# Moving waits inside the tiles of a two-layer recurrent decoder step, and sharing its two ends with GpSimd

## The chip, the cores and the metric

The kernel runs on one core of a Trainium2 chip. The metric is device time in microseconds (us), the median of several executions. All data starts and ends in HBM.

## The reference, cut to what matters

One inference step of a two-layer decoder trunk runs for a prompt of 512 tokens and for 8 samples of 4 tokens, 544 tokens in all, with model width 1024 in float32. Each layer adds half a SwiGLU block, then a mixer, then half a SwiGLU block:

```python
x = x + 0.5 * _swiglu(_rmsnorm(x, norm_ffn1), w_ffn1_in, w_ffn1_out)          # width 2816
xn = _rmsnorm(x, norm_mix)
(mq, mk, mv, mo, mg_if, gq, gk, gv, gg, glr, lx, ly, mgate) = _split_cols(xn @ w_in)
h_ml, C1, n1, m1 = _mlstm(q, k, v, log_i, log_f, C0, n0, m0)                  # 4 heads, chunks
y_ml = _head_layernorm(h_ml, g_ml_norm) * sigmoid(mo)
o_gla, S1 = _gla(gq_, gk_, gv_, _heads(log_a, GLA_HEADS), S0)                 # 4 heads
y_gla = _head_rmsnorm(o_gla, g_gla_norm) * silu(gg)
xc, cb1 = _causal_conv(lx, cb0, w_conv, b_conv)
h_lru, h1 = _rglru(xc, w_lru_a, b_lru_a, w_lru_i, b_lru_i, lru_lambda, h0, pos)
y_lru = h_lru * gelu(ly)
merged = gm[:, :, 0] * y_ml + gm[:, :, 1] * y_gla + gm[:, :, 2] * y_lru       # gm = sigmoid(mgate)
x = x + merged @ w_out
x = x + 0.5 * _swiglu(_rmsnorm(x, norm_ffn2), w_ffn2_in, w_ffn2_out)
```

A last RMSNorm follows. All recurrent states are outputs too.

## The kernel before, in words

Activations lie transposed: 8 feature tiles (k) of 128 partitions by 544 tokens. A weight block of 128x2048 is loaded by SyncE's queue into one of two slots of `stage`; ScalarE (ACT) writes its rounded high part `wh` (L776), VectorE (DVE) writes the rest `wl` (`split_lo`, L1075), and the block is free for the next load. TensorE (PE) makes a product of high and low parts in three passes (L393). `tile` (L399 on) runs 8 k-steps of 6 matmuls into one of two PSUM pairs, `stream_a` and `stream_b`; DVE evicts a tile with `take` (L1066, L1068), which multiplies by `rstd`, the reciprocal norm, and so can run only when the norm of the tokens is done. A tile of the same pair may start only after that eviction. PSUM `mix` (Q, 4 banks) holds all small products.

Every engine's order is written out by hand, and semaphores join them. `link` makes DVE wait for its own last instruction. Per layer, in this order:

- **ffn** (two halves of up and down tiles). After it comes the **gate block** (`gate_block`, `gate_rows`, L1176 on): a tile of gate columns, the column sums of squares (`norm_squares`, L425), and then `q`, `k` and value tiles of the first head. DVE evicts the gate tile with `rstd`.
- **mLSTM heads** (`mlstm_head`), 4 of them. Near the end of a head PE runs `mean` (`column_sum`, L520, which waits for `a_h`, the sum `wS`) between k-steps 2 and 3 of the last tile, then the variance sum (L520 on `hsq`, which waits for `square_sum`, L1281) after it. ACT's `head_root` (L866) follows, and `merge_head` (L1288 to L1295) in the next head.
- **GLA heads** (`gla_head`), 4 of them. The first starts with `decays` (L615), which waits for the last mLSTM head's root. DVE turns 14 slices `seven` into factors (L1433) once ACT has made the exponentials, and takes the values (L1219) in the middle of that. At the end of a head PE runs `sample_updates` (L513) and the variance sum after the last tile, waiting for `square_sum`.
- **LRU pairs** (`lru_pair`), 4 of them: convolution (L1509 to L1530), gates (L719), a scan (`recur`), GeLU branch (`take_y`), and `merge` (L1578 to L1582) of the pair before. Its state inputs reuse memory of the heads, so their loads wait until the last GLA state is stored.
- **out blocks**, 4 of two tiles, which read `mh` and `ml`, the merged result; k-steps wait for `m_ready`.
- **ffn** again. After layer 2: last norm (L425, L806, L1099), 8 scalings (L1640) and 8 stores.

At the start ACT makes high parts and squares of x in turn, DVE low parts and the running sum `acc`, with the first two weight blocks' parts between them; GpSimd (POOL) sets constants and issues 21 small loads. The layer loop of PE is a hardware loop (`Fori`).

## Time and profile before

| | us |
|---|---|
| median of 3 executions | 3292.69 (3290.55 to 3293.36) |
| the profiled execution | 3291.07 |
| its span, first to last instruction | 3288.9 |
| PE busy, 24,724 matmuls | 3155.8 (96%) |
| DVE busy | 1929.6 (59%) |
| ACT busy | 1027.3 (31%) |
| GpSimd busy | 11.4 (0%) |

PE is the bound nearly everywhere: what the other engines do counts only where PE waits for them, at the start before its first matmul and at the end after its last. The profile also gives the clock that PE was granted: 0.98 of full speed over the span, with stretches at half speed.

### The profile page before, as it was taken

Reading aid. Unit: us, or ns where it says so; the run is one execution under the profiler, and the core shown is the slowest. Engines: PE = TensorE matmul, PEld = TensorE weight load, DVE = VectorE, ACT = ScalarE, POOL = GpSimd, SP = SyncE. Lnnn points to the kernel's source line nnn. Section 1 sums busy time; section 2 is a strip of 40 time slices with the busy share of each in tenths; the row PEclk is TensorE's granted clock in tenths of the full one; section 3 lists DMA queues with packets and bytes.
Section 4 is the critical chain, followed back from the end, with each engine's and each line's share of the span. In section 5 each row is a group of like instructions: output and inputs, shape, how many; then the busy total and the mean of one; then the engine's idle time right before and its main releaser. Section 6 shows DMA issues by size and latency. Waiting matters only on the chain.

```text
span 3288.9 us, 58471 instructions
## 1 busy us (share of the span) xinstructions
PE 3155.8 (96%) x24724; PEld 3098.9 (94%) x24724; DVE 1929.6 (59%) x2653; ACT 1027.3 (31%) x983; POOL 11.4 (0%) x33
## 2 busy tenths in 40 slices
PE   7999989999999999999999999999999999999997
PEld 7999989989889989999999999899898899899997
DVE  5434467667777875434454345666777788654344
ACT  3222232333334543212232123232333346421122
POOL 1000000000000000000000000000000000000000
PEclk9999999999999999999999999999999999999999
DMA  4232232322222222222222223232222222222221
GB/s 143 80 102 81 78 106 94 126 92 79 79 91 75 83 79 81 77 98 84 83 90 85 99 80 99 77 136 91 92 79 78 86 89 77 77 90 83 96 75 67
DMA packets 52021, 292.53 MB, mean 89 GB/s; under 512 B 9480, under 2 KB 12296, under 8 KB 23992
## 3 DMA queue, kind: packets, MB, share of 16 engines
q1 hardware_dynamic: 37440, 243.60, 22.2%
q10 hardware_dynamic: 13696, 46.32, 3.9%
q8 instruction: 86, 1.41, 0.2%
q0 software_dynamic: 768, 0.95, 0.1%
q14 instruction: 31, 0.25, 0.0%
HBM read 269.33 MB, written 21.50 MB: 88 GB/s over the span
## 4 chain that ended last, share of the span: by engine, by line
PE 67%; DVE 18%; ACT 8%; issue 3%; DMA 3%; DVEq 0%; ACTq 0%; SPq 0%
PE stream_b L393 30%; PE stream_a L393 30%; PE stream_a L467 3%; ACT wh L776 2%; DVE wl L1075 2%; DMA out_o_ss<-CS 2%; DVE hsq L1288 2%; DVE xc L1524 1%; DVE seven L1433 1%; PE stream_b L467 1%; PE mix L647 1%; DVE tg L1360 1%; DVE tg L1066 1%; ACT L987 1%; DVE Cst L1264 0%
## 5 line engine op out<-in xcount | busy, mean ns | idle before, releaser
L776 ACT ACTIVATE wh<-stage 128x2048 fp32r<-128x2048 f32 (+2 forms) x246 | 436.0, 1772 | 837.6 <-PE stream_b L393 549.3
L1075 DVE TENSOR_TENSOR wl<-stage,wh 128x2048 fp32r<-128x2048 f32 (+2 forms) x248 | 525.9, 2120 | 161.3 <-ACT wh L776 144.9
L393 PE MATMUL stream_a<-xh,wh 128*128 128x272 f32 x2560 | 542.5, 294 | 29.6 <-DVE wl L1075 15.8
L393 PE MATMUL stream_b<-xh,wh 128*128 128x272 f32 x2560 | 537.2, 291 | 9.3 <-DVE lyg L1066 7.0
L393 PE MATMUL stream_a<-xh,wl 128*128 128x272 f32 x2560 | 534.8, 291 | 0.0
L393 PE MATMUL stream_a<-xl,wh 128*128 128x272 f32 x2560 | 532.8, 290 | 0.0
L393 PE MATMUL stream_b<-xh,wl 128*128 128x272 f32 x2560 | 528.7, 288 | 0.0
L393 PE MATMUL stream_b<-xl,wh 128*128 128x272 f32 x2560 | 527.7, 287 | 0.0
L393 PEld LDWEIGHTS stream_a<-xh,wh 128*128 128x128 f32 x2560 | 408.8, 192 | 34.2 <-issue 19.2
L393 PEld LDWEIGHTS stream_b<-xh,wh 128*128 128x128 f32 x2560 | 402.4, 188 | 17.4 <-DVE lyg L1066 7.8
L393 PEld LDWEIGHTS stream_a<-xh,wl 128*128 128x128 f32 x2560 | 408.8, 191 | 0.0
L393 PEld LDWEIGHTS stream_a<-xl,wh 128*128 128x128 f32 x2560 | 406.2, 191 | 0.0
L393 PEld LDWEIGHTS stream_b<-xh,wl 128*128 128x128 f32 x2560 | 402.7, 189 | 0.0
L393 PEld LDWEIGHTS stream_b<-xl,wh 128*128 128x128 f32 x2560 | 400.3, 189 | 0.0
L1066 DVE TENSOR_TENSOR us<-stream_b,rstd 128x544 f32<-128x544 f32 x88 | 63.8, 725 | 446.2 <-PE stream_b L393 446.2
L827 ACT ACTIVATE sg<-gs 128x544 f32<-128x544 f32 x88 | 57.9, 658 | 398.2 <-DVE gs L1066 398.2
L467 PE MATMUL stream_a<-wh,xh 128*128 128x256 f32 x512 | 144.6, 282 | 6.1 <-DVE qT L1066 6.1
L393 PE MATMUL stream_b<-hh,wh 128*128 128x272 f32 x704 | 146.1, 289 | 0.0
L393 PE MATMUL stream_a<-hh,wh 128*128 128x272 f32 x704 | 146.0, 289 | 0.0
L467 PE MATMUL stream_a<-wh,xl 128*128 128x256 f32 x512 | 145.4, 284 | 0.0
L393 PE MATMUL stream_a<-hh,wl 128*128 128x272 f32 x704 | 145.3, 287 | 0.0
L393 PE MATMUL stream_b<-hh,wl 128*128 128x272 f32 x704 | 145.2, 287 | 0.0
(331 smaller groups left out, 4586.5 us busy)
## 6 DMA issues: line engine op xcount, KB each, us to landing
stage<-in_w_up SPq DMA_DIRECT2D x88, 1024.0 KB, 4.9
stage<-in_w_mix SPq DMA_DIRECT2D x88, 1024.0 KB, 4.9
stage<-in_w_down SPq DMA_DIRECT2D x32, 768.0 KB, 4.3
stage<-in_w_down SPq DMA_DIRECT2D x32, 640.0 KB, 3.9
CS<-in_c ACTq DMA_DIRECT2D x8, 1024.0 KB, 4.7
out_o_sc<-CS ACTq DMA_DIRECT2D x8, 1024.0 KB
CS<-in_s ACTq DMA_DIRECT2D x8, 1024.0 KB, 4.9
out_o_ss<-CS ACTq DMA_DIRECT2D x8, 1024.0 KB
```

What stands on the lines that cost most here:

```text
L393: mm = [pe.matmul(out(h), a(h), b(h), start=f, stop=z) for h in range(2)]
L467: mm = pe.matmul(out, a[:, k, tok:tok + C], b[:, j, k * DV:(k + 1) * DV], start=f, stop=z)
L647: mm = pe.matmul(Q[:, q, sl], lhs, rhs, start=True, stop=True)
L776: act.activation(wh[:, slot, 0:width], stage[:, slot, 0:width], ACT.Copy).then_inc(hi_done, 1)
L827: act.activation(sg[:], gs[:], ACT.Silu).then_inc(silu_done, 1)
L987: act.activation(lyg[:, v, :], lyg[:, v, :], ACT.Gelu_apprx_tanh).then_inc(l_act, 1)
L1066: ins = tt_(halves(dst), banks(pair[slot]), rs2, ALU.mult)
L1075: tt_(wl[:, slot, 0:width], stage[:, slot, 0:width], wh[:, slot, 0:width].bitcast(F32), ALU.subtract).then_inc(split_done, 1)
L1288: link(dve.reciprocal(hsq[:, 1, :], hsq[:, 1, :]))
L1360: link(dve.reciprocal(tg[:], tg[:]))
L1433: tt_(ev[:, :, a, :], ev[:, :, a, :], sv[:, :, a, :], ALU.mult)
L1524: stt(xc[:, j, 0:T], lxp[:, j, a:a + T], w[a], xc[:, j, 0:T], ALU.mult, ALU.add)
```

## The change

It keeps the mathematics and moves work:

- **Start.** Both halves of x load on ACT's queue. ACT makes the high part of weight block 0 first, then high parts and squares in groups, and block 1's high part last. DVE makes block 0's low part first and then all 8 low parts of x; the squares of k 0 to 3 are summed by GpSimd, which also makes block 1's low part. The norm's column sums move into the middle of the second tile. `ones` is set by GpSimd instead of loaded.
- **Gate block.** DVE copies the gate tile raw to `sq` before the norm is known, clears `val` and `Kf` while it waits, and takes `q` before the gate logarithms are back. ACT makes the next block's high part before the rows' store.
- **Heads.** In `mlstm_head` one `split_lo` moves behind `a_h`, `mean` runs ahead of the last tile, and the variance sum after its k-step 5; ACT's root runs before the last gate. The reciprocal of `merge_head` becomes `invert_root` and moves to the next head's start (mLSTM) or ahead of the wait for the exponentials (GLA). In `gla_head` the merge moves ahead of the second gate, a `split_lo` behind the states, `evictions` into the third gate, and three `sample_updates` and the variance sum into the last tile.
- **LRU.** `take_y(1)` runs before `recur(0)`. In the last pair of a layer each half is merged as soon as it is ready, and `split(4)` comes last.
- **End.** No high and low parts are made in the last ffn. ACT scales rows 0 to 2 of x by the final weight and loads the square root's table early; GpSimd multiplies these three rows by `rstd`, DVE the other five.
- PE's layer loop is written out for both layers.

The diff, cut to its core:

```diff
@@ gpsimd
+            for e, m in enumerate((1, 2, 3)):
+                pool.wait_ge(sq_ready, m + 1)
+                pool.tensor_tensor(first_sum, first_sq[0] if m == 1 else first_sum, first_sq[m], ALU.add).then_inc(first_half, 1)
...
+            pool.tensor_tensor(wl[:, 1, :], stage[:, 1, :], wh[:, 1, :].bitcast(F32), ALU.subtract).then_inc(split_done, 1)
...
+            pool.wait_ge(last_norm, 1)
+            for m in range(3):
+                pool.tensor_tensor(x[:, m, :], y_part[m][:], rstd[:], ALU.mult).then_inc(y_pool, 1)
@@ tensor, mlstm_head
-                pair_block(n + 3, t + 6, 1, None, ((), ((2, mean), (7, third))))
-                pe.wait_ge(a_sqs, B + 1)
-                column_sum(hsq[:, 0], 0, a_var)
+                pair_block(n + 3, t + 6, 1, mean, ((), ((5, variance), (6, third))))
@@ tensor, gla_head
-                pair_block(n + 3, t + 6, 1, outputs)
-                pe.wait_ge(b_sqs, B + 1)
-                sample_updates(1, 2, b_us)
-                pe.wait_ge(head_samples, taken + 1)
-                sample_updates(2, 3, b_us)
-                column_sum(hsq[:, 0], 0, b_var)
+                def second():
+                    pe.wait_ge(b_h, B + 1)
+                    sample_updates(1, 2, b_us)
+
+                def third():
+                    pe.wait_ge(b_sqs, B + 1)
+                    column_sum(hsq[:, 0], 0, b_var)
+                    pe.wait_ge(head_samples, taken + 1)
+                    sample_updates(2, 3, b_us)
+
+                pair_block(n + 3, t + 6, 1, outputs, ((), ((4, second), (6, third))))
@@ tensor
-            with pe.Fori(0, DEPTH) as L:
+            for L in range(DEPTH):
@@ scalar, mlstm_head
+                act.wait_ge(a_var, B + 1)
+                head_root()
                 next(gates, None)
                 split_hi(nh + 2, 1, t + 7, 2 * D)
-                act.wait_ge(a_var, B + 1)
-                head_root()
@@ vector, gla_head
                 split_lo(n + 2, 0, 2 * D)
+                invert_root(number - 1)
                 dve.wait_ge(b_exp, B + 1)
...
+                merge_head(HEADS - 1 if first else i - 1, first)
                 take_gate(L, i, t + 5, 1, 1, acts + 1, "silu", None)
-                split_lo(n + 4, 0, 2 * D)
@@ vector, lru_pair
+                take_y(1)
+                recur(0)
+                if not last:
...
+                else:
+                    take(t + 4, 0, tt[:, 0])
+                    split(3)
+                    merge(0)
+                    take(t + 5, 1, last_branch)
+                    recur(1)
+                    merge(1)
+                    split(4)
```

PE, the end of a GLA head of the middle (`xh,wh`, `xl,wh` and `xh,wl` matmuls of `stream_b` are its last tile, `mix<-V4,Kws` the sample updates, `mix<-hsq,ones` the variance sum; what waits stands in brackets). Before:

```order
L393 MATMUL stream_b<-xh,wh 128x272 x2
L393 MATMUL stream_b<-xh,wl 128x272 x2
L393 MATMUL stream_b<-xl,wh 128x272 x2
L513 MATMUL mix<-V4,Kws 128x256 [waits b_square_sum]
L513 MATMUL mix<-V4,Kws 128x256
L700 ISA
L513 MATMUL mix<-V4,Kws 128x256 [waits head_samples]
L513 MATMUL mix<-V4,Kws 128x256
L520 MATMUL mix<-hsq,ones 128x272 x2
L703 REGISTER_ALU
L513 MATMUL mix<-V4,Kws 128x256 [waits head_samples]
```

And now, from k-step 4 of that tile on:

```order
L544 MATMUL mix<-V4,Kws 128x256 [waits b_h]
L544 MATMUL mix<-V4,Kws 128x256
L410 MATMUL stream_b<-xh,wh 128x272 x2
L410 MATMUL stream_b<-xh,wl 128x272 x2
L410 MATMUL stream_b<-xl,wh 128x272 x2
L410 MATMUL stream_b<-xh,wh 128x272 x2
L410 MATMUL stream_b<-xh,wl 128x272 x2
L410 MATMUL stream_b<-xl,wh 128x272 x2
L551 MATMUL mix<-hsq,ones 128x272 [waits b_square_sum]
L551 MATMUL mix<-hsq,ones 128x272
L738 REGISTER_ALU
L544 MATMUL mix<-V4,Kws 128x256 [waits head_samples]
```

The wait for the squares stood after all 8 k-steps and now stands after 6, with a wait for `b_h` ahead of k-steps 5 and 6.

DVE, the middle of an mLSTM head, from the eviction of its second gate tile to that of its third (`wl<-stage,wh` is the low part of the next weight block, `wS<-Hh` the sum that PE's `mean` waits for). Before:

```order
L1066 TENSOR_TENSOR tg<-stream_b,rstd 128x544 [waits tile_done]
L1075 TENSOR_TENSOR wl<-stage,wh 128x2048 [waits hi_done,gate_act,tile_free]
L1358 SCALAR_TENSOR_TENSOR tg<-mix,seven 128x512 [waits a_denominator]
L1359 TENSOR_TENSOR tg<-tg,mix 128x512 [waits dve_chain]
...
L1366 TENSOR_TENSOR Hh<-mix,tg 128x2x512 [waits a_out,dve_chain]
L1367 TENSOR_TENSOR wS<-Hh 128x544 [waits dve_chain]
L1066 TENSOR_TENSOR tg<-stream_a,rstd 128x544 [waits tile_done]
```

And now:

```order
L1128 TENSOR_TENSOR tg<-stream_b,rstd 128x544 [waits tile_done]
L1435 SCALAR_TENSOR_TENSOR tg<-mix,seven 128x512 [waits a_denominator,gate_act,tile_free]
L1436 TENSOR_TENSOR tg<-tg,mix 128x512 [waits dve_chain]
...
L1443 TENSOR_TENSOR Hh<-mix,tg 128x2x512 [waits a_out,dve_chain]
L1444 TENSOR_TENSOR wS<-Hh 128x544 [waits dve_chain]
L1137 TENSOR_TENSOR wl<-stage,wh 128x2048 [waits hi_done]
L1128 TENSOR_TENSOR tg<-stream_a,rstd 128x544 [waits tile_done]
```

The low part of the weights moved from ahead of the denominator to between `wS` and the third gate tile.

## Rows read from the trace of the kernel before

**Rows 1.** PE's waits: us in total, times, longest us.
```profile
PE mix L513 <- DVE hsq L1281: 33.4, 8, 5.0
PE stream_a L393 <- DVE wl L1075: 15.8, 1, 15.8
PE mix L520 <- DVE wS L1367: 10.7, 6, 1.9
PE stream_a L393 <- DVE ml L1582: 10.5, 4, 3.5
PE stream_a L393 <- DVE val L1219: 9.2, 5, 4.3
PE mix L615 <- ACT hsq L866: 8.5, 2, 4.3
PE stream_b L393 <- DVE lyg L1066: 7.0, 4, 1.8
PE stream_a L467 <- DVE qT L1066: 6.1, 2, 3.1
...
PE stream_b L393 <- DVE xg L1183: 2.3, 2, 1.2
```

**Rows 2.** Windows behind long waits: length, busy (count) by engine, PEclk, DMA; sums.
```profile
866.00:869.93 3.93, 3.93 (x13) 3.46 (x14) 2.47 (x5) 3.87 (x5) 0.00 (x0) 0.50 0.00 0
...
sum 38.31, PE 38.30 PEld 34.57 DVE 29.02 ACT 36.18 POOL 0.00; mean PE 4.79 PEld 4.32 DVE 3.63 ACT 4.52 POOL 0.00
...
sum 11.11, PE 11.11 PEld 11.11 DVE 8.63 ACT 3.47 POOL 0.00; mean PE 3.70 PEld 3.70 DVE 2.88 ACT 1.16 POOL 0.00
...
sum 12.10, PE 12.10 PEld 10.45 DVE 5.83 ACT 3.15 POOL 0.00; mean PE 6.05 PEld 5.22 DVE 2.91 ACT 1.57 POOL 0.00
...
sum 18.61, PE 15.03 PEld 14.40 DVE 12.82 ACT 2.59 POOL 0.00; mean PE 7.52 PEld 7.20 DVE 6.41 ACT 1.29 POOL 0.00
```

**Rows 3.** Timeline of the start: start, duration, instruction, idle before and releaser.
```profile
0.91 0.15 POOL L360 MEMSET pick<- 128x64 f32 x1
...
11.28 1.91 ACT L793 ACTIVATE wh<-stage 128x2048 fp32r<-128x2048 f32 x1 [0.94 <-DMA stage<-in_w_up]
...
27.31 1.08 PE L425 MATMUL mix<-acc,ones 128*128 128x272 f32 x4
...
33.35 0.72 DVE L1066 TENSOR_TENSOR gs<-stream_a,rstd 128x544 f32<-128x544 f32 x1 [0.38 <-DVE rstd L1099]
```

**Rows 4.** Timeline of the gate block, DVE.
```profile
461.18 2.29 DVE L1075 TENSOR_TENSOR wl<-stage,wh 128x2048 fp32r<-128x2048 f32 x1 [10.19 <-ACT wh L776]
```

**Rows 5.** Timeline of the second mLSTM head, ACT.
```profile
636.79 1.11 ACT L909 ACTIVATE hsq<-Hh 128x1088 f32<-128x1088 f32 x1 [2.45 <-DVE Hh L1371]
```

**Rows 6.** Timeline of the first two GLA heads, DVE.
```profile
740.24 1.23 DVE L1219 TENSOR_TENSOR val<-stream_a,rstdT 128x1024 f32<-128x1024 f32 x1 [1.53 <-PE stream_a L467]
...
853.73 3.55 DVE L1288 RECIPROCAL hsq<-hsq 128x544 f32<-128x544 f32 x1
```

**Rows 7.** Timeline where a layer's LRU pairs begin and end, DVE.
```profile
1038.87 0.18 DVE L1514 COPY lxs<-cv 128x24 f32<-128x24 f32 x1 [3.54 <-DMA cv<-in_conv]
...
1190.89 1.29 DVE L1546 TENSOR_TENSOR_SCAN hseq<-xg,ii 128x544 f32<-128x544 f32 x1
...
1204.28 0.72 DVE L1582 TENSOR_TENSOR ml<-tt,mh 128x544 fp32r<-128x544 f32 x1
```

**Rows 8.** Timeline of the end, ACT and DVE.
```profile
3271.06 0.64 ACT L815 ACTIVATE sq<-x 128x544 f32<-128x544 f32 x1
...
3274.89 1.28 ACT L806 ACT_TABLE_LOAD   x1 [3.19 <-PE mix L425]
...
3280.76 5.66 DVE L1640 SCALAR_TENSOR_TENSOR x<-x,vectors,rstd 128x544 f32<-128x544 f32 x8
```

**Rows 9.** DMA queue (packets, MB, share) and an issue (KB each, us to landing).
```profile
q8 instruction: 86, 1.41, 0.2%
...
vectors<-in_vec SPq DMA_DIRECT2D x1, 112.0 KB, 2.3
```

More of the change, by code:

```diff
@@ L293, in trunk @@
         rr, aa = sd, (sq, xg)
-        first_sq = (sq, xg)
+        last_branch = xc[:, 0, :]
+        first_sq = [merged[:, m, :] for m in range(KT)]
+        first_sum = qT[:]
+        y_part = (gs, us, sg)
+        raw = sq
         def halves(ap):
@@ L360, in _ @@
             pool.memset(pick[:], 0.0)
+            pool.memset(ones[:], 1.0)
             pool.memset(one_t[:], 1.0).then_inc(split_done, 2)
@@ L410, in tile @@
                         late(k_tiles - 1 - k)
+                    if low is not None:
+                        pe.wait_ge(low, k + 1)
                     if fresh is not None:
@@ L426, in norm_squares, with first_block @@
                 return mm
+            def first_block(n, t, j, norm):
+                parts = (wh[:, j], wl[:, j])
+                block_ready(n)
+                tile(t, 0, KT, 2 * P, 0, weights=parts, low=first_low)
+                tile(t + 1, 1, KT, 2 * P, P, weights=parts, ks=range(KT // 2))
+                pe.wait_ge(acc_ready, norm)
+                norm_squares().then_inc(norm_sum, 1)
+                tile(t + 1, 1, KT, 2 * P, P, weights=parts, ks=range(KT // 2, KT))
             def ffn_in_block(L, n, t, j, norm=None):
+                if norm == KT:
+                    return first_block(n, t, j, norm)
                 block_ready(n)
@@ L599, in mean, with variance @@
                     sample_updates(1, 3, a_us)
+                def variance():
+                    pe.wait_ge(a_sqs, B + 1)
+                    column_sum(hsq[:, 0], 0, a_var)
                 def third():
@@ L843, in down @@
                             if half == 1:
-                                squares(i * 2 + (t + j), i * 2 + j, g_col + i * 2 + j)
+                                squares(i * 2 + (t + j), i * 2 + j, g_col + i * 2 + j, not last)
                             if width:
@@ L967, in lru_pair, with branch, gates @@
                 t = L * LAYER_TILES + i * 12 + (TILE_MIX + GATE_TILES + 2 * HEADS * HEAD_TILES + 6 * j2)
-                def gates(j):
+                def branch(v, buf):
+                    tile_taken(t + 4 + v)
+                    act.activation(buf, buf, ACT.Sigmoid).then_inc(l_act, 1)
+                def gates(j, between=None):
                     k = pr * 2 + j
@@ L1046, in _ @@
             chain.end()
+            for m in range(3):
+                high = (DEPTH - 1) * V_COLS + V_NEXT + m
+                act.wait_ge(h_done, DEPTH * 2 * sum(FF_HALVES))
+                act.activation(y_part[m][:], x[:, m, :], ACT.Copy,
+                               scale=V[:, high:high + 1]).then_inc(xh_ready, 1)
+            act.activation(sdT[:], sdT[:], ACT.Sqrt)
             norm_root(3 * DEPTH)
@@ L1138, in down @@
                             if half == 1:
-                                prepare(i * 2 + j, g_col + i * 2 + j, norm * KT + i * 2 + (KT + j))
+                                prepare(i * 2 + j, g_col + i * 2 + j, norm * KT + i * 2 + (KT + j), not last)
                             if width:
@@ L1589, in mix @@
                 dve.wait_ge(tile_free, L * LAYER_TILES + (TILE_MIX + 3))
+                tile_ready(L * LAYER_TILES + (TILE_MIX + 1))
+                dve.tensor_copy(halves(raw[0:80]), banks(pair[1])[0:80]).then_inc(tile_free, 1)
+                dve.wait_ge(tile_free, L * LAYER_TILES + (TILE_MIX + 4))
+                chain.restart()
+                link(dve.memset(val[:, :, DV:DV + P], 1.0))
+                link(dve.memset(val[:, NC, 0:DV], 0.0))
+                link(dve.memset(Kf[:], 0.0))
                 reciprocal_norm(L * 3 + 1)
```

193 lines of the change are left out of this document (109 added, 84 removed).

## The prediction

> **What bounds the kernel now.** I read the busy times first: PE works for 96% of the span, so an edit pays only where PE stands still or runs slowly. The next view is PE's waits [rows 1]. The nine rows sum to 103.5 us, from a few places that repeat per head or per layer: 33.4 us in eight waits for the sum of squares at the end of a GLA head, 10.7 in six waits of `mean` in an mLSTM head, 8.5 in two for the root before `decays`, 17.6 in the gate block and the values behind it, and 17.5 among the LRU pairs and the out blocks. Third, windows laid behind the long waits [rows 2]. The reader is to see the granted clock in the first one: 0.50, the 1.2 GHz level, although PE is busy throughout. Behind each wait of about 3 us or more PE shows such a stretch, behind the waits of under 2 us in the heads none. So a long wait costs its length and half of the busy time behind it: 38.31/2 = 19.2 us behind the eight GLA waits, 11.11/2 = 5.6 in the gate block, 12.10/2 = 6.0 behind `decays`. By PE's busy time over its 24,724 matmuls (0.128 us each) a k-step, which is 6 matmuls, takes 0.75 us at full clock, a tile 6.0, and I take 1.4 for a k-step at half. Last I read the timelines of the places that the change touches, engine by engine [rows 3 to 8], and followed each new order of DVE, ACT and PE with the durations of those rows. Against the profiled execution (3291.07 us) the sum is:
>
> **A, the start: +1.1.** Before, block 0 landed at 11.28 and ACT wrote `wh` at once, since its table had been loaded under x [rows 3]. Now the table load (1.28, as in [rows 8]) and `wh` (1.9) follow the landing, then DVE's low part (2.29 [rows 4]) and the first low part of x (0.8): PE starts at 17.6 instead of 15.8 [rows 1]. Twelve k-steps later, three of them at half clock, the norm's column sums start at 28.4 instead of 27.31. From there to the first eviction it took 6.04 us [rows 3]; the third tile waits for that, so the delay of 1.1 stays. If block 0 lands between the halves of x, 2.6 us sooner, this is -1.5; if x and the block share the queue badly, +3. Block 1's low part goes to GpSimd; its only price here is a memset of 64 columns in 0.15 us [rows 3], or 4.8 us for 2048 columns, and it has over 10 us until block 1 is used.
>
> **B, the gate block: -21.3.** The raw copy frees the tile's PSUM without the norm, and `q` is taken before the rows are ready. The waits for xg (2.3), qT (6.1) and the values' eviction (4.3 and 3.0 of the 9.2) go [rows 1], and 5.6 of half clock [rows 2]: 15.7 + 5.6. The clears of `val` and `Kf` fill the time in which DVE waits for the norm, and ACT's `wh` no longer stands behind the rows, for which DVE's low part waited 10.19 us [rows 4]. In my replay `q` is out 9 us before PE needs its slot and the values in time.
>
> **C, mLSTM heads: +4.2.** The low part (2.29) and its wait move behind `wS`, so `mean` loses its 10.7 us [rows 1]. But the variance sum moves from behind k-step 8 to behind k-step 5. Behind `wS` DVE and ACT need: low part 2.29 [rows 4], and, as each operation over 544 columns takes about 0.7 [rows 7, 8], eviction, sigmoid and product with two hand-overs 1.65 from the eviction's start, centring 1.35 (two of them), square 1.11 [rows 5], square sum 0.73: 7.1. PE needs 1.5 for `mean` and 5 x 0.75 for the k-steps, 5.3, and arrives about 1.86 us early, in all eight heads: +14.9 - 10.7. None of these waits is long enough for half clock. Queued behind the waiting sum are three k-steps and `third`, which has slack. Bounds: 0 (DVE is quicker, -10.7 in all) and 3.0 a head with half clock behind it (+20).
>
> **D, `decays` and the first GLA head: -2.1.** ACT's root now runs ahead of the last gate, so the 8.5 us go [rows 1] and 6.0 of half clock [rows 2]. What is late next: DVE in that head has the reciprocal (3.55 [rows 6]) ahead of the exponentials, which it formerly had later. Before, DVE waited 1.53 us for the values' tile at 740.24 [rows 6]; now PE is about 4.3 us earlier, while DVE has 3.55 more to do and only its 2.3 of idle time ahead of the factors to cover it. The eviction comes some 4.2 us late, in each layer, with about 2.0 of half clock: +12.4. Bounds 0 and 6 a layer.
>
> **E, the GLA heads: -54.5.** The variance sum moves from behind k-step 8 to behind k-step 6, which sounds like a later wait for PE, but DVE's squares move further: the merge, with its reciprocal of 3.55 [rows 6] and two products, leaves the place just ahead of the third gate tile, the `split_lo` too. In the replay the squares are ready at 65.6 us of a head and PE asks for them at 67.8. All 33.4 us go [rows 1], 19.2 of half clock [rows 2], and 1.9 of the waits for the values in the heads of the middle (0.80, 0.64 and their like in layer 2). The margin of the values' eviction there is thin, 0.25 us.
>
> **F, LRU and out blocks: -9.6.** Here a chain over DVE and ACT sets the time of a pair, PE has slack. (1) The last GLA state is stored some 2.2 us later against PE, and the loads of the pairs start behind it; DVE waited 3.54 for them already [rows 7]: +2.2. (2) `take_y(1)` stands ahead of `recur(0)`: +0.76 for three pairs. (3) In the last pair 12.8 us lay between the end of the last scan (1190.89 + 1.29) and the end of the second `ml` (1204.28 + 0.72) [rows 7]. Now one merge of 3.75 follows it; merge(0) stands ahead of the scan with one eviction, 3.75 + 0.76 less an idle 2.4: the scan ends 2.1 later. So `ml` is ready 6.65 earlier, and PE has 1.9 less to do behind it (one k-step of two tiles instead of two). Per layer 2.2 + 2.3 - 8.55 = -4.1, two layers -8.1. PE was busy 15.03 us at half clock there [rows 2]; 1.5 of it goes with the waits for `ml` (10.5 [rows 1]), while those for `lyg` (7.0) stay or grow. Bounds: -22 (all waits for `ml` and their half clock) and 0.
>
> **G, the end: -3.4.** No high part: ACT's square, which ended at 3271.70 [rows 8], is 0.65 earlier. ACT then scales three rows (3 x 0.65) and loads the table (1.28 [rows 8]) beside PE's sums; the root starts at 3274.65, not 3276.18: -1.5. DVE scales five rows, not eight, of 0.70 each (5.66/8 [rows 8]): -2.1. GpSimd has three products in the same time. Their price by the memset is between 0.6 us (a fixed 0.1 and 0.9 ns a column) and 1.3 (0.15/64 a column); at 1.3 the three take 3.8 instead of 3.5: +0.2.
>
> **PE's written-out loop: 0.** No wait of PE's shows the engine looking for instructions.
>
> Sum: 1.1 - 21.3 + 4.2 - 2.1 - 54.5 - 9.6 - 3.4 = -85.6, so 3205.5 against the profiled execution. The median of the runs is 1.6 above that execution: **3207 us**.
>
> **The rivals.** *GpSimd and DVE exclude each other.* If a product with two inputs in SBUF on one of them stops the other, the eight scalings at the end run one after the other, 5 x 0.70 + 3 x 0.6 to 1.3, or 5.3 to 7.4 for the 5.66 of before, and the start's sums and low part stretch by 1 or 2: 3207 + 3.5 = **3210.5**. For it: both use the same memory at the same time, against it: nothing in this trace, where GpSimd does no such work. The Trainium skill, page "SBUF — State Buffer", section "Who interferes with whom", speaks against this part of the change: a DVE instruction with two inputs in SBUF contends with a GpSimd instruction that reads it, through a port pair that one of them locks. No row here can show it. Chance 0.2.
>
> *DVE becomes the bound of the GLA heads.* With PE's 8 us a head gone, DVE is left with 0.25 us of margin at the values. If each operation costs a few ns more than I counted, a wait of 2 us appears in six heads, with 1.3 of half clock: +20, **3227**. For it: the values' waits of before (0.80, 0.64); against it: the replayed order still has idle time in DVE. Chance 0.13.
>
> *The new waits of C, D and F do not appear*, because PE meets them later than replayed: -14.9 (I keep 4), -12.4 (I keep 8): **3192**. Chance 0.13.
>
> *PE's code is fetched too late*, the slower side. The layer loop is written out, so PE passes through twice the code. The instruction queue carried 86 packets [rows 9]. If every packet of as many new ones stalls PE for a small load's time to landing, 2.3 us [rows 9], that is 198 us: **3403**. It decides from 85.6/86 = 1.0 us a packet on, above which the kernel is slower than before. Against it: the inner loops remain, and the long written-out stretches of PE today show no such gap. The Trainium skill, page "Runtime: NRT & Kernel Launch", section "Instruction fetch mechanics", holds the other way: streaming ahead is mostly hidden, and taken branches break it. The trace agrees as far as it goes, with no wait of that kind. Chance 0.02.
>
> *A part does not do what it says*: the long waits of the GLA heads return elsewhere, half of E is lost, 3207 + 27 = **3234**. Chance 0.04.
>
> **How the numbers follow.** The forecast's own case has 0.48, with bounds from A (-2.6 to +1.9), C (-10 to +10), D, F (-5 to +5), about 12 either way together. To 8 in 10 the range takes in the cases of GpSimd, of DVE's bound and of the waits that do not appear: **3186 to 3230**. What a measurement of this kernel can tell from no change is about 0.2%, 6.6 us. All cases but the slower side lie far under 3286: faster 0.96, same 0.02, slower 0.02.
>
> **What would show it.** PE's waits of the changed kernel should have no line for the sample updates behind `hsq`, none for xg or qT, eight waits of about 1.9 us at the variance sum of the mLSTM heads, two of about 4 at the values of the first GLA heads, waits for `lyg` as before and none or short ones for `ml`. PE's first matmul comes at 17.6. Windows in the GLA heads should show a granted clock of 1.0. At the end five scalings of DVE stand beside three products of GpSimd, and their durations, against 0.70, tell whether the two exclude each other. I would be wrong if PE's total wait were above 60 us, if a GLA head took over 72 us instead of 70.5 (78.5 before), or if PE showed gaps without a releaser.

## The result, and the profile after

The changed kernel takes 3237.72 us (median of 4 executions, 3237.12 to 3239.91); the kernel before takes 3291.62 (4 executions beside them). The ratio is 0.9838, 95% interval 0.9821 to 0.9855: 1.6% faster. The forecast was 3207, with a range of 3186 to 3230. The sign is right, the time lies 7.7 us above the range, and of the 85.6 us that were forecast 53.7 came.

| | before | after |
|---|---|---|
| the profiled execution | 3291.07 | 3237.12 |
| its span | 3288.9 | 3235.2 |
| PE busy | 3155.8 | 3134.7 |
| PE's idle time before its last matmul | 119.0 | 84.7 |

The page's busy times after the change:

```profile
PE 3134.7 (97%) x24724; PEld 3083.5 (95%) x24724; DVE 1928.0 (60%) x2638; ACT 1034.0 (32%) x987; POOL 26.5 (1%) x40
```

PE's waits after the change (us in total, times, longest):

```profile
PE stream_a L410 <- DVE xl L1143: 18.6, 2, 17.9
PE stream_a L410 <- DVE val L1292: 15.4, 8, 4.2
PE mix L551 <- DVE hsq L1356: 14.9, 8, 2.1
PE stream_b L410 <- DVE tt L1128: 6.8, 4, 2.2
PE stream_a L410 <- DVE lxs L1587: 6.5, 2, 3.2
PE stream_a L410 <- DVE x L1157: 5.6, 4, 2.7
PE mix L443 <- DVE acc L1237: 3.1, 1, 3.1
PE stream_a L410 <- DVE gs L1128: 2.5, 1, 2.5
...
PE stream_a L410 <- DVE ml L1654: 1.4, 2, 0.7
```

Beside [rows 1] the reader sees what the change does: the lines of 33.4, 10.7, 8.5, 6.1 and 2.3 us are gone, and that of `ml` is down from 10.5 to 1.4. In their place stand the variance sum of the mLSTM heads (14.9, eight times, as forecast), the values in eight GLA heads where two were forecast (15.4), and the waits of LRU and out blocks for `tt`, `lxs` and `x` (18.9 together), of which the forecast had little; the 7.0 us for `lyg`, which it left standing, are gone. PE's whole idle time of 84.7 us lies above the 60 that the prediction named as a sign of being wrong, and a middle GLA head takes 71.6 us from value tile to value tile, where it had 70.5.

PE's order of tile matmuls is the same in both kernels, so the start of the same tile in both traces can be subtracted. These differences, cut at the borders of the stages, give the sum as measured (a border can be drawn a few tenths of a us to either side):

| term | forecast | measured |
|---|---|---|
| A, start, to the third tile | +1.1 | +7.05 (34.24 to 41.29) |
| B, gate block, two layers | -21.3 | -20.1 |
| C, mLSTM heads 1 to 3 | +4.0 | +5.8 |
| C to E, last mLSTM head, `decays`, GLA heads | -56.4 | -47.8 |
| F, LRU and out blocks | -9.6 | +3.2 |
| turn of the layer loop | 0 | -1.8 |
| G, end | -3.4 | -0.05 |
| sum | -85.6 | -53.7 |

### The profile page after: what moved, and what is told of

Its sections match the earlier page's. It is cut to its first block, busy times and chain, and to the rows that moved or that the text cites. A ratio compares the mean times of both kernels' runs of the same rounds, so it can differ in the third digit from the quotient of the medians.

```text
span 3235.2 us, 58231 instructions
## 1 busy us (share of the span) xinstructions
PE 3134.7 (97%) x24724; PEld 3083.5 (95%) x24724; DVE 1928.0 (60%) x2638; ACT 1034.0 (32%) x987; POOL 26.5 (1%) x40
## 4 chain that ended last, share of the span: by engine, by line
PE 71%; DVE 17%; ACT 6%; issue 3%; DMA 3%; DVEq 0%; ACTq 0%; POOL 0%; SPq 0%; POOLq 0%
PE stream_b L410 32%; PE stream_a L410 30%; DVE wl L1137 2%; PE stream_a L497 2%; DMA out_o_ss<-CS 2%; ACT wh L817 1%; DVE hsq L1362 1%; DVE seven L1512 1%; DVE tg L1437 1%; DVE xc L1602 1%; PE mix L680 1%; ACT L1038 1%; DVE tg L1128 1%; PE mix L551 1%; PE stream_b L497 1%
## 5 line engine op out<-in xcount | busy, mean ns | idle before, releaser
L410 PE MATMUL stream_a<-hl,wh 128*128 128x272 f32 x704 | 145.1, 287 | 0.0
L410 PE MATMUL stream_b<-hl,wh 128*128 128x272 f32 x704 | 145.0, 287 | 0.0
```

Source lines behind the costliest of these rows:

```text
L410: mm = [pe.matmul(out(h), a(h), b(h), start=f, stop=z) for h in range(2)]
```

## The experiments

Unless said otherwise, each is the changed kernel (3237.72 us) with the edit shown, and stands on one profiled execution; the differences by stage come from subtracting tile starts as above. At places that follow a stretch of half clock, steps of about 1.6 us come and go between runs whose code is the same there, so totals of single runs are read to about 2 us and the places by themselves.

### Start on DVE alone, and the end one engine after the other

```diff
-            for e, m in enumerate((1, 2, 3)):
-                pool.wait_ge(sq_ready, m + 1)
-                pool.tensor_tensor(first_sum, first_sq[0] if m == 1 else first_sum, first_sq[m], ALU.add).then_inc(first_half, 1)
...
-            pool.tensor_tensor(wl[:, 1, :], stage[:, 1, :], wh[:, 1, :].bitcast(F32), ALU.subtract).then_inc(split_done, 1)
@@ start, vector
+            for m in range(1, KT):
+                dve.wait_ge(sq_ready, m + 1)
+                ins = tt_(acc[:], first_sq[0] if m == 1 else acc[:], first_sq[m], ALU.add)
...
+            split_lo(1, 1, 2 * D)
@@ end, vector
+            dve.wait_ge(y_pool, 3)
             for m in range(3, KT):
```

> The changed kernel with two edits far apart. Start: GpSimd's three sums and its low part of block 1 are made by DVE. End: DVE waits until GpSimd's three products are done and only then scales its five rows. Theory A (an instruction of GpSimd and one of DVE that both read two inputs in SBUF exclude each other): at the start the low parts of x take 0.79 us each instead of 1.13, no sum takes 5 us, and the third tile starts near 36.4 instead of 41.29, so about -4.9; at the end GpSimd's products take clearly less than the 1.8 us of the changed kernel, about 1.1 to 1.3, and DVE's 0.70. Theory B (GpSimd is simply slow and DVE waits for its results, without exclusion): DVE's low parts stay at 1.13 us, the third tile starts at 39 or later, and GpSimd's products stay at 1.8 us alone.

Measured: 3236.75 us. The third tile starts 5.15 us sooner. Of this 1.5 are lost again at once: PE waits 2.76 us ahead of that tile instead of 2.48, and the 4.5 us behind the wait are at a granted clock of 0.62 instead of 1.00; 2.8 are left at the last tile. At the end 2.3 us are lost to the waiting. First the changed kernel's rows, DVE and GpSimd at the start (start, duration, instruction, idle time before):

```profile
16.97 9.03 DVE L1143 SCALAR_TENSOR_TENSOR xl<-x,vectors,xh 128x544 fp32r<-128x544 f32 x8
...
26.67 5.74 DVE L1235 TENSOR_TENSOR acc<-acc,merged 128x544 f32<-128x544 f32 x2
...
26.08 4.99 POOL L377 TENSOR_TENSOR wl<-stage,wh 128x2048 fp32r<-128x2048 f32 x1 [1.35 <-issue]
```

and at its end:

```profile
3225.16 6.79 DVE L1734 SCALAR_TENSOR_TENSOR x<-x,vectors,rstd 128x544 f32<-128x544 f32 x5
3225.28 1.86 POOL L399 TENSOR_TENSOR x<-gs,rstd 128x544 f32<-128x544 f32 x1 [3183.97 <-DVE rstd L1730]
3227.11 1.80 POOL L399 TENSOR_TENSOR x<-us,rstd 128x544 f32<-128x544 f32 x1
```

The same in this run, start and end:

```profile
17.16 5.66 DVE L1137 SCALAR_TENSOR_TENSOR xl<-x,vectors,xh 128x544 fp32r<-128x544 f32 x8
...
23.49 4.58 DVE L1229 TENSOR_TENSOR acc<-acc,merged 128x544 f32<-128x544 f32 x6
...
3223.78 1.32 POOL L393 TENSOR_TENSOR x<-us,rstd 128x544 f32<-128x544 f32 x1
...
3226.50 3.57 DVE L1731 SCALAR_TENSOR_TENSOR x<-x,vectors,rstd 128x544 f32<-128x544 f32 x5 [4.17 <-POOL x L393]
```

Alone, a product of GpSimd takes 1.32 us and a scaling of DVE 0.71 (3.57 for five). Side by side the products take 1.80 to 1.86, and of the five scalings the three that meet a product take 1.85 each, the first and the last 0.78 (the records of one instruction overlap the next by some 0.07). The two sums in 5.74 us are not stretched alike: the one that starts at 26.67, while GpSimd makes the low part of block 1 (26.08 to 31.07), takes 4.98 us, the next one 0.72. Without GpSimd six take 4.58. Three of the eight low parts of x, too, take 1.88 to 1.95 us beside GpSimd's sums, the other five 0.78. Theory A holds. The three products and five scalings one after the other are 3.96 + 3.57 = 7.53 us of work, together they took 6.79, and DVE had made eight in 5.66 [rows 8]. So GpSimd's help is worth less than nothing here. The Trainium skill, page "SBUF — State Buffer", section "Who interferes with whom", calls the port pair that the two engines share "an exclusive lock". The trace agrees: the sum of 4.98 us ends 0.58 us behind GpSimd's low part. That 6.79 is under 7.53 shows that a little of two such instructions is still overlapped.

### CS loaded behind the exponentials, and the end on DVE alone

```diff
@@ scalar, gla_head
-                act.wait_ge(state_stored, stored)
-                act.dma_start(CS[:], s0[L, i]).then_inc(b_cs, 16)
                 split_hi(nh + 1, 0, t + 1, 2 * D)
                 act.wait_ge(b_diff, B + 1)
...
                 act.activation(kh[:], kh[:], ACT.Exp, scale=inv).then_inc(b_exp, 1)
+                act.wait_ge(state_stored, stored)
+                act.dma_start(CS[:], s0[L, i]).then_inc(b_cs, 16)
@@ end, vector
-            for m in range(3, KT):
+            for m in range(KT):
```

At the end the three scaled rows of ACT and the three products of GpSimd go; the early load of the square root's table stays.

> The changed kernel with two edits far apart. GLA heads: ACT's wait for the stored state and its load of the next CS move from ahead of the high part of the weights to behind the four exponentials. End: DVE scales all 8 rows, GpSimd none. Theory A (the waits for the values in the second to fourth GLA heads, 2.0, 0.9 and 0.8 us a layer, come from ACT's queue, which stands still for the store before it makes wh, after which DVE's low part, reciprocal and factors follow): DVE's low part starts up to 3.7 us earlier and all six waits vanish, -7.1 us; the first heads' waits of 4.1 stay or shrink. Theory B (DVE's own work is the bound there): the waits stay within 0.5 us. End, by exclusion: 8 scalings in 5.66 instead of 6.79, and the end about 1.3 us shorter; without exclusion it would be longer, as three rows more are on DVE.

Measured: 3220.64 us, 17 us less. In the changed kernel the second GLA head reads, ACT and then DVE:

```profile
792.88 0.35 ACTq L1007 DMA_DIRECT2D out_o_ss<-CS  x1
803.02 0.33 ACTq L980 DMA_DIRECT2D CS<-in_s  x1
803.46 1.92 ACT L817 ACTIVATE wh<-stage 128x2048 fp32r<-128x2048 f32 x1 [12.10 <-DMA out_o_ss<-CS]
...
805.41 2.29 DVE L1137 TENSOR_TENSOR wl<-stage,wh 128x2048 fp32r<-128x2048 f32 x1 [3.70 <-ACT wh L817]
...
813.30 1.22 DVE L1292 TENSOR_TENSOR val<-stream_a,rstdT 128x1024 f32<-128x1024 f32 x1
```

and in this run:

```profile
798.50 1.92 ACT L812 ACTIVATE wh<-stage 128x2048 fp32r<-128x2048 f32 x1 [7.00 <-PE stream_b L405]
...
801.99 2.29 DVE L1127 TENSOR_TENSOR wl<-stage,wh 128x2048 fp32r<-128x2048 f32 x1
...
3210.48 5.66 DVE L1724 SCALAR_TENSOR_TENSOR x<-x,vectors,rstd 128x544 f32<-128x544 f32 x8
```

The store of the last state, 10 us from issue to landing, held up ACT's whole queue, `wh` among it; with the load moved, `wh` is made 5 us sooner and DVE does not wait for it. The line of the values in PE's waits goes from 15.4 us in eight to 8.6 in two, those of the first heads: six waits vanish, as theory A said. By the tile starts the heads give 13.7 us, about twice the 7.1 of the waits alone. The granted clock behind these waits was 1.00, so half clock is not the rest; it comes at the level matmuls behind them (L680 of the changed kernel), where six more waits for DVE, 2.0 us in all, go too, and in smaller steps around them. The end is 3.0 us shorter than the changed kernel's: 1.1 by the scalings, 1.2 because ACT no longer has three rows to scale ahead of the table and the root, and 0.7 between the last scaling and the end of the last store.

### The reciprocal at the merge again

```diff
@@ vector, gla_head
                 split_lo(n + 2, 0, 2 * D)
-                invert_root(number - 1)
                 dve.wait_ge(b_exp, B + 1)
...
+                invert_root(number - 1)
                 merge_head(HEADS - 1 if first else i - 1, first)
```

> The changed kernel with the reciprocal of the root back just ahead of the merge in the GLA heads. Theory A (the 3.55 us reciprocal ahead of the factors is what makes the values late): the waits for the values of 4.1 us in the two first GLA heads shrink to under 0.7, with some 2 us of half clock each, and those of the later heads vanish: together -18 us, unless the reciprocal makes the merge and the squares late, which would show as a wait at the variance sum or the sample updates in the last tile. Theory B (the values wait for something else, the exponentials of ACT): the waits stay above 3 us in the first heads.

Measured: 3246.41 us, 9 us more. PE's waits:

```profile
PE mix L530 <- DVE seven L1464: 13.1, 6, 2.9
PE stream_a L410 <- DVE val L1292: 10.7, 8, 2.4
```

The first heads' waits for the values shrink from 4.2 to 2.4 (2.2 in layer 2), not to under 0.7: the reciprocal is only part of it. In the later heads the 3.55 us delay the states, and the sample outputs (L530) wait for them. What stands ahead of the values in the first head is then ACT: DVE waits 1.54 us for the last of the exponentials, and six of its factors come before the eviction. The place of the change is the better one in three heads of four, the worse one in the first.

### The variance sum behind k-step 7

```diff
-                pair_block(n + 3, t + 6, 1, mean, ((), ((5, variance), (6, third))))
+                pair_block(n + 3, t + 6, 1, mean, ((), ((6, third), (7, variance))))
```

> The changed kernel with the variance sum of the mLSTM heads behind k-step 7 of the last tile instead of 5 (the third sample update stays behind 6). Theory A (PE is early at k-step 5 by 1.9 us and only the place is at fault): two k-steps of 0.75 cover 1.5 of 1.86, eight waits of 0.4 remain, -12 us, and nothing is late behind it. Theory B (the root that follows then is late for the next head's reciprocal or for the decays, or the sum waits for DVE wherever it stands): less than -6 us.

Measured: 3222.21 us, 15.5 us less. The line of `hsq` in PE's waits is gone altogether; in layer 1 each head is 1.74 us shorter, no line of waits is new (that of `ml` is 2.8 us instead of 1.4), and the first GLA heads wait 4.7 for the values instead of 4.2, since PE comes sooner. Even the 0.4 us that theory A left do not show. The 14.9 us of C were a choice of place, not a price of the new order.

### The state stored first, acc cleared early

```diff
@@ vector, gla_head (last head)
-                split_lo(n + 5, 1, 2 * D)
                 sample_states(eb, 3, 2, b_us, B, number)
+                split_lo(n + 5, 1, 2 * D)
@@ vector, mix
                 link(dve.memset(lxp[:, :, 0:3], 0.0))
+                link(dve.memset(acc[:], 0.0))
...
-                clear_acc()
```

> The changed kernel with two edits in the LRU part. In the last GLA head DVE updates the last sample states ahead of the low part of the weights, so that ACT can store the state sooner, behind which the pairs' loads wait; and acc is cleared ahead of the pairs instead of between the last merge and the first residual of the out blocks. Theory A (the LRU part starts late because the store is issued late, and the out blocks wait for work of DVE behind the last merge): the store is issued about 1.2 us sooner, as ACT's root is then the last thing ahead of it, the wait at lxs shrinks from 3.2 to about 2.0, and the wait at x in the out block from 2.65 to 1.6: -4 to -6 us in the two layers with their half clock. Theory B (the store takes until another transfer is done, whenever it is issued): the wait at lxs stays at 3.2.

Measured: 3234.39 us, 3 us less, of which the tile starts put 1.8 at the two places of the edit. The store is issued at 1004.66 instead of 1006.30 and the loads behind it at 1014.69 instead of 1015.83, although this run is 1.4 us behind the changed kernel here; DVE's wait for the loads (`lxs<-cv`) falls from 3.04 to 0.59 us. The store took 10.0 us instead of 9.5; a 1 MB weight block is loaded at the same time in the changed kernel, and the two move 2.1 MB in those 9.5 us. What the store would take by itself no run shows.

PE's wait at `lxs`, however, goes only from 3.2 to 3.0, and neither theory has the reason. The changed kernel's rows of DVE show it, and one of ACT (the issue of the first load):

```profile
1003.19 2.29 DVE L1137 TENSOR_TENSOR wl<-stage,wh 128x2048 fp32r<-128x2048 f32 x1 [1.02 <-ACT wh L817]
...
1007.80 3.55 DVE L1362 RECIPROCAL hsq<-hsq 128x544 f32<-128x544 f32 x1 [0.21 <-DVE Hh L1571]
...
1012.71 1.29 DVE L1372 TENSOR_TENSOR merged<-merged,Hh 128x1088 f32<-128x1088 f32 x1
...
1015.02 0.18 DVE L1587 TENSOR_TENSOR lxs<-stream_a,rstd 128x32 f32<-128x32 f32 x1
1018.24 0.18 DVE L1592 COPY lxs<-cv 128x24 f32<-128x24 f32 x1 [3.04 <-DMA cv<-in_conv]
...
1015.83 0.35 ACTq L1081 DMA_DIRECT2D h0t<-in_h  x1
```

PE waits from 1012.02 to 1015.25 for L1587, the last piece of the first LRU tile's eviction. That ends before the loads are even issued, so it can't wait for them: ahead of it stands the merge of the last GLA head, with its reciprocal, and DVE is busy nearly without a pause. The loads hold up DVE only behind it (L1592), where PE does not wait. In this run DVE no longer waits 1.0 us for `wh`, since the states come first, but the clearing of `acc` stands ahead of the eviction and takes 0.7 of it back. The wait at `x` goes from 2.65 to 2.0, half of what was expected.

### The eviction of the GeLU branch behind the scan

```diff
-                take_y(1)
+                if last:
+                    take_y(1)
                 recur(0)
                 if not last:
+                    take_y(1)
                     split(3)
```

> The changed kernel with the eviction of the second GeLU branch behind the first scan again in the three first LRU pairs of a layer, as before the change. Theory A (the pairs are set by the chain over DVE and ACT, and that eviction stands in it): each of three pairs is 0.76 us shorter, -4.6 in all, and the waits for lyg of 1.7 us come back in place of those for tt. Theory B (PE's wait for lyg is what the order was changed for, and weighs more): the pairs are longer by 0.5 to 1 us each, +3 to +6.

Measured: 3230.50 us, 7 us less. The LRU pairs and the out blocks are 3.0 and 2.7 us shorter in the two layers, 0.9 to 1.0 a pair. The waits for `tt` (6.8) are gone, one for `lyg` of 1.75 a layer is back. The rest of the 7 us comes up at places where the code is the same. The eviction stands in the chain that sets a pair's time, as the forecast had it (0.76 a pair).

### The start of before, and PE's loop

In the first of two runs ACT again makes high part and square of each row in turn and DVE low part and sum, with block 0 behind row 1 and the norm sums behind the first tile. The second also has

```diff
@@ tensor
-            for L in range(DEPTH):
+            with pe.Fori(0, DEPTH) as L:
```

> The changed kernel with the start of the kernel before: x on two queues, high part, square, low part and sum in turn on ACT and DVE, block 0 between them, norm sums behind the first tile, no arithmetic on GpSimd. Theory A (the new start is what costs 7.05 us at the third tile, in three parts: the first matmul 2.07 later, GpSimd and DVE excluding each other 4.9): the third tile starts at 34.24 again, and the whole run is 7 us shorter than the changed kernel. Theory B (part of it comes back later, since block 1 is ready earlier or later): the whole run differs from the start by over 1 us.

> Run e7 (the changed kernel with the start of before), with PE's layer loop as a hardware loop again. Theory A (the written-out loop costs and gives nothing): the run stands within 1.5 us of e7's 3229.25, no stage between the third tile and the end moves by over 0.5 us apart from steps of about 1.6 us that follow half clock. Theory B (it hides a fetch or costs one): a step of 1 us or more at the end of layer 1 or within layer 2.

Measured: 3229.25 us without and 3229.02 with the loop. With the old start the third tile starts 6.82 us sooner and the last tile 8.1: the new start costs what it seemed to and gives nothing back later; the 1.3 us more at the last tile are within the steps of half clock. The loop's run has a wait that the other has not, at the first matmul of layer 2:

```profile
1615.49 0.79 PE L405 MATMUL stream_a<-xh,wh 128*128 128x272 f32 x2 [2.01 <-issue]
```

The kernel before has it too, at the same matmul, where the profile puts it down to DVE:

```profile
1646.06 0.52 PE L393 MATMUL stream_a<-xh,wh 128*128 128x272 f32 x2 [1.72 <-DVE x L1088]
```

So the one turn of the hardware loop costs PE 1.7 to 2.0 us here, and writing the loop out gives that once. In the totals it is lost: the loop's run had about 4 us less of waits for the values. The rival in which the written-out code starves PE is refuted; the changed kernel's waits of PE have no line at issue. The Trainium skill, page "Runtime: NRT & Kernel Launch", section "Instruction fetch mechanics", names taken branches as what breaks the fetching ahead. The gap at the branch, and none in the straight code, agree with it; that the gap is a fetch no row says.

### The reciprocal behind the factors

```diff
                 split_lo(n + 2, 0, 2 * D)
-                invert_root(number - 1)
...
                 dve.memset(t8[:], 0.0).then_inc(b_fac, 1)
                 split_lo(n + 3, 1, 2 * D)
+                invert_root(number - 1)
```

with the load of CS as above.

> Run e2's edit in the GLA heads (ACT's load of CS behind the exponentials), without its end, and the reciprocal of the root not ahead of the factors but behind them and the next low part, ahead of the fifth gate tile, where DVE had 1.7 us of idle time. Theory A (in the first GLA head of a layer only the place of the reciprocal makes the values late, and this place has idle time): the values' waits of 4.2 vanish with 2 us of half clock each, and against e2 the heads are 10 to 12 us shorter. Theory B (the 3.55 us delay the ring of levels, the merge and the states, as in the run with the reciprocal at the merge): waits of 1.5 to 3 us appear at the level matmuls or at the sample outputs, in all heads, and the gain is gone.

Measured: 3253.02 us, 15 us more than the changed kernel. PE's waits:

```profile
PE mix L680 <- DVE wS L1529: 21.6, 8, 3.7
...
PE stream_a L410 <- DVE val L1292: 4.4, 2, 2.2
```

The values' waits in the first heads are halved, and in all eight heads the level matmuls now wait 2.1 to 3.7 us for DVE. The 1.7 us of idle time at that place were no slack: the ring of levels begins there, and everything behind it moves. Theory B.

### The last pair of a layer as before

```diff
                 else:
-                    take(t + 4, 0, tt[:, 0])
                     split(3)
-                    merge(0)
-                    take(t + 5, 1, last_branch)
+                    take(t + 4, 0, tt[:, 0])
                     recur(1)
-                    merge(1)
+                    take(t + 5, 1, tt[:, 1])
                     split(4)
+                    merge(0)
+                    merge(1)
```

ACT's order of the branches and PE's wait ahead of two k-steps follow it.

> The changed kernel with the last LRU pair of a layer as before the change: both merges behind both scans and behind the last low part, and PE waits for them ahead of the last two k-steps. Theory A (the two-step merge gives 6.65 + 1.9 us at the second ml and costs 2.65 and half clock at the next residual, which waits for the low part behind it): the pair and the out blocks are 9 to 11 us longer up to the second ml, the wait for x of 2.65 is gone, and the net is +4 to +7 a layer. Theory B (the two-step merge gives nothing net): within 1 us a layer.

Measured: 3248.45 us, 11 us more. Up to the end of the first two out tiles, where the second `ml` has been used, the layers are 9.9 and 10.0 us longer, behind the out blocks 5.1 and 5.4. In the last pair and the out blocks of layer 1 and the ffn behind, PE's waits are

```profile
PE stream_a L410 <- DVE ml L1652: 5.8, 2, 3.5
PE stream_b L410 <- DVE tt L1128: 4.6, 2, 2.5
```

and the one for `x` is gone. So merging in two steps gives 9.9 us a layer up to `ml`, where the forecast had 8.55, and costs 4.6 behind it, where the forecast had nothing: 5.3 are left. Theory A holds in every part.

### All that paid, together

The start of before, the end on DVE alone with the table loaded early, the load of CS behind the exponentials, the reciprocal at the merge in the first GLA head only, the variance sum behind k-step 7, the state stored first and acc cleared early, and the GeLU eviction behind the scan.

> All that paid so far in one: start of before, the end on DVE alone with the square root's table loaded early, CS loaded behind the exponentials in the GLA heads, the reciprocal of the root at the merge in the first GLA head alone, the variance sum of the mLSTM heads behind k-step 7, the last GLA state updated first, acc cleared early, the eviction of the GeLU branch behind the scan. Theory A (the costs are separate, so they add): 3237.7 - 8 - 3 - 13.5 - 14 - 2.7 - 6.6 - 4 = about 3186, range 3180 to 3196. Theory B (one engine, DVE, stands behind them all, so that what is taken away at one place comes back at the next): above 3200, with the waits for the values back at over 1 us in the middle GLA heads.

Measured: 3181.69 us (4 executions, 3178.05 to 3182.51), ratio to the kernel before 0.9663, interval 0.9647 to 0.9679: 3.4% faster, twice what the change gave. The costs add. PE's largest waits:

```profile
PE stream_a L400 <- DVE wl L1117: 15.9, 1, 15.9
PE stream_a L400 <- DVE lxs L1571: 6.0, 2, 3.0
PE stream_a L400 <- DVE val L1270: 5.7, 2, 2.9
PE stream_a L400 <- DVE x L1137: 4.2, 4, 1.9
PE stream_a L400 <- DVE ml L1638: 3.3, 2, 1.6
```

What is left beyond the start is the merge of the last GLA head ahead of the LRU pairs (`lxs`), the first GLA heads and the last merge.

> Run e10 with the reciprocal of the root ahead of the factors in the first GLA head too, as in the changed kernel. Theory A (that reciprocal is what makes the values late there, and its place at the merge makes nothing else late in that head): the waits for the values of 4 to 4.7 us are back in the two first GLA heads, each head 4 to 5 us longer with its half clock, +8 to +10 in all. Theory B (ACT's exponentials set that time, and the reciprocal lies under the wait for them): within 3 us in all.

Measured: 3187.26 us, 5.6 more. The values' line reads 9.4 us in two waits instead of 5.7. Up to the next head the two first heads are 1.7 and 1.2 us longer; the rest of the 5.6 comes up around the LRU parts, where the code is the same. For the heads themselves theory B is nearer: the reciprocal's place is worth about 1.5 us a head.

## Why the prediction was wrong

The orders were followed rightly at nearly every place, and one of the two largest new lines of waits was named to the tenth. That is in part luck: its eight waits were each forecast at 1.86 and measured 1.7 to 2.1. Of the 31.9 us that were missing, 30.8 are in four terms, A, E, F and G.

**A, the start: 6 us missed.** The first matmul came at 17.89, forecast 17.6. But "from there to the first eviction" was reckoned from column sums at 28.4, and they came at 33.3: the step that failed is the price of GpSimd's part, "it has over 10 us until block 1 is used". What counted was not when its result is needed but that a sum of DVE, on the path, stands still meanwhile (4.98 us for 0.72), as three low parts had before. The last 1.1 us are the column sums themselves, 2.18 us instead of 1.08, behind a wait of 3.14. GpSimd's duration was estimated well (4.8, measured 4.99 beside DVE's work). The rival had this mechanism, with a chance of 0.2, but priced it at the start at 1 or 2 us.

**G, the end: 3.4 us missed.** The same rival, at the place where it was named: 6.79 us for five scalings, inside its 5.3 to 7.4. The root came 1.8 us earlier against the last tile, as forecast; the scalings took 1.1 of it back where 2.1 less were forecast, and the last store ends 3.2 us behind the last scaling instead of 2.5.

**B: right** (-20.1 for -21.3).

**C: right in mechanism and size** for the waits (14.9 for 14.9), +1.8 in small new waits of the first mLSTM head, where `Kw` and the states come 0.5 to 1.0 us after PE asks. What it did not see is that the place could be chosen at no cost; the run with the sum behind k-step 7 shows it.

**D: right in mechanism.** The first GLA heads wait 4.16 and 4.10 for the values, forecast 4.2. Its reason was half right: the runs with the reciprocal elsewhere leave 2.2 to 2.9 of it. With the reciprocal away, what stands there is the wait for the exponentials and the factors. Up to the first GLA head about 2 us of the 8.6 that C to E miss together are gone already, most of it in layer 2; no run follows them.

**E: about 6.5 us missed.** Six waits for the values in the middle and last heads (2.0, 0.8 and 0.8 a layer) are 7.15. The forecast had them gone, with a "margin of the values' eviction" of 0.25 us, and the rival with DVE as the bound had a wait of 2 us in each of the six. The mechanism was neither. The step that failed is that margin: it holds only if ACT's high part comes when PE's tile is done, and ACT's queue stood for the store that takes 10 us, whatever PE does. PE's heads became 7 us shorter (78.6 to 71.6), the store did not. The run that moves the load shows it, and its 13.7 us are more than the miss, so the rest of E came out better than forecast.

**F: 12.8 us missed**, +3.2 where -9.6 was forecast. (1) The start: 3.3 and 4.9 us in the two layers, half clock included, for 2.2. The sign is right and the reason wrong. The term took DVE's wait for the loads [rows 7] as the price; the loads did come later against PE, but PE does not wait for them. What failed is "PE has slack" at the eviction ahead: PE comes there without its former wait of 3.6 for the squares, DVE's merge of the last GLA head is as long as before, and PE waits 3.2. (2) `take_y(1)`: 3.6 us a layer for 2.3, as PE then runs at half clock for part of the time behind a wait of 2.2; the run that moves it back gives 3.0 and 2.7, which shows sign and cause. The waits for `lyg` did not "stay or grow" but went. (3) The last pair: the gain up to `ml` was there, 10.1 us a layer in the differences, 1.9 of it by the wait for `lyg`. The forecast's own terms give 6.95 for the part that it has as 6.65 (12.8 - 3.75 - 2.1). But the low part that was put behind the last merge now stands ahead of the first residual:

```profile
1181.10 2.29 DVE L1137 TENSOR_TENSOR wl<-stage,wh 128x2048 fp32r<-128x2048 f32 x1
...
1184.78 0.72 DVE L1157 SCALAR_TENSOR_TENSOR x<-stream_a,x 128x544 f32 x1 [0.49 <-DVE acc L1163]
```

PE waits 2.65 for it, 3.4 with half clock, and up to the end of the out blocks 3.9 and 4.2 are lost. The forecast named no work that is late next there, which is the step that failed.

**PE's loop: 1.8 us the other way.** "No wait of PE's shows the engine looking for instructions" was wrong: the 1.72 at the turn of the layers was in the trace, under another engine's name.

**The clock: right in kind.** PE's busy time over the same 24,724 matmuls fell by 21.1 us; the sum had 28.3 (19.2 + 5.6 + 6.0 + 1.5, less 4.0 behind the new waits). The difference fits the stretches of half clock behind the waits that the sum did not have. Behind the remaining wait of 4.2 in layer 1 the clock is at its lower level, as the first of these windows shows, behind the first GLA head's wait (length, busy and count of PE, PEld, DVE, ACT, POOL, granted clock, DMA share, GB/s):

```profile
740.80:745.00 4.20, 4.17 (x18) 4.20 (x19) 4.17 (x11) 0.00 (x0) 0.00 (x0) 0.50 0.00 0
814.50:818.60 4.10, 4.03 (x32) 4.03 (x33) 4.07 (x11) 1.34 (x2) 0.00 (x0) 1.00 0.00 0
1015.00:1019.50 4.50, 4.25 (x21) 4.25 (x22) 1.38 (x6) 1.77 (x1) 0.00 (x0) 0.62 0.43 135
1185.50:1190.00 4.50, 4.44 (x23) 4.44 (x24) 2.15 (x4) 1.95 (x4) 0.00 (x0) 0.62 0.63 239
```

In layer 2 the window behind the 4.1 us (2335.8 to 2340.0) has 0.61. Behind the 2.0 us of the second head the clock is not at the lower level; behind 3.2 at `lxs` and 2.65 at `x` the lower level takes part of the window.

**The range.** 12 us either way for the forecast's own case was too little: the misses of A, E, F and G all had one sign, that of work which was reckoned as covered. Two of the rivals, GpSimd's contention and the waits for the values, were set up as alternatives with small chances each, and came together.

## What to carry to other kernels

When a stage becomes faster, look at what on the helping engines does not become faster with it, above all a wait for a DMA in a queue that also holds the next tile's inputs: behind it stands everything else that engine has to do. A sum that PE waits for is put where its inputs are ready; here two k-steps later cost nothing. A wait that ends before a transfer is issued is not a wait for that transfer: compare the two times before the DMA is blamed. Before GpSimd is given part of DVE's work, count the time as the sum of both, not as the longer; here the scalings took 1.1 us more at the end, and the third tile came about 5 us later at the start. An idle stretch ahead of a chain was no room for more work here.

## What the runs showed of the hardware

- Products over 128x544 with both inputs in SBUF take GpSimd 1.32 us and DVE 0.71 apart, 1.80 to 1.86 and 1.85 side by side. A sum of DVE of 0.72 us that met a GpSimd instruction of 4.99 us took 4.98.
- A store of 1 MB beside a load of 1 MB took 9.5 to 10.1 us from its issue to that of the load which waits for it.
- A turn of PE's hardware loop over a long body cost 1.7 to 2.0 us, and the profile put it down to "issue" in one run and to DVE in another.
- The granted clock over the 4 to 4.5 us behind a wait was 0.50 behind 4.2 us (0.61 behind 4.1 in layer 2), 0.62 behind 3.2 us at `lxs`, behind 2.65 us in the out blocks and behind 2.15 us at `tt`, and 1.00 behind 2.0 us in a GLA head.
